# RWKV-7/Hyena block step: the scan's triangular inverse accumulates in PSUM over its levels, and Gram and output matmuls alternate between the two heads of a block

## What is computed

```python
def step(s, inp):
    r_t, w_t, k_t, v_t, kk_t, a_t = inp
    sa = jnp.einsum('bhvk,bhk->bhv', s, -kk_t)
    s = (s * w_t[:, :, None, :] + sa[..., :, None] * (kk_t * a_t)[..., None, :]
         + v_t[..., :, None] * k_t[..., None, :])
    return s, jnp.einsum('bhvk,bhk->bhv', s, r_t)
```

## Time and profile before

| | |
|---|---|
| Runs of the kernel before | 2445.35, 2448.92, 2464.73 us (median 2448.92) |
| Profiled execution: span | 2456.2 us (its own time is known only as this span, 7.3 us above the median) |
| Mean granted TensorE clock | 0.908 of full speed |
| PE busy | 2161.2 us, 88% of the span |
| PE weight load busy | 1846.5 us, 75% |
| DVE busy | 1120.2 us, 46% |
| ACT busy | 816.9 us, 33% |
| First layer's scan | about 204 to 620 us |
| Second layer's scan | about 1071 to 1466 us |
| L802, seeds of GM | 96 matmuls of 512 columns |
| L807, seeds of DM | 80 matmuls of 512 columns |

### The profile page before, as it was taken

The page is one execution under the profiler, slowest core; times in us unless marked ns, Lnnn a source line. Parts: engine busy times, 40 slices in busy tenths (PEclk is TensorE's granted clock), DMA queues, the critical chain, the costliest instruction groups (busy, mean ns, idle before and its releaser), DMA issues. The chain is left out here.

```text
span 2456.2 us, 31677 instructions
## 1 busy us (share of the span) xinstructions
PE 2161.2 (88%) x13765; PEld 1846.5 (75%) x13765; DVE 1120.2 (46%) x1369; ACT 816.9 (33%) x957; POOL 114.9 (5%) x161
## 2 busy tenths in 40 slices
PE   7888999989677998878888886778999999999996
PEld 2386776766566997768777774668899899898895
DVE  0154443232556554633444435654455454454554
ACT  0143232333223443332323323224333343343343
POOL 2001100010002000010101100000000000000000
PEclk9997999999798999856789887979999999999998
DMA  9831232232315555310101012234555655555552
GB/s 293 270 110 35 87 104 87 87 104 88 120 35 164 178 188 176 112 34 18 35 27 45 20 51 69 69 103 138 192 168 172 197 174 181 183 168 191 176 169 89
DMA packets 247418, 301.31 MB, mean 123 GB/s; under 512 B 8427, under 2 KB 224080, under 8 KB 247152
## 3 DMA queue, kind: packets, MB, share of 16 engines
q1 hardware_dynamic: 240112, 286.28, 36.4%
q0 software_dynamic: 4192, 11.28, 1.5%
q10 hardware_dynamic: 2976, 1.73, 0.2%
HBM read 297.69 MB, written 1.57 MB: 122 GB/s over the span
## 5 line engine op out<-in xcount | busy, mean ns | idle before, releaser
L1326 DVE TENSOR_TENSOR WL<-WRING,WH 128x2048 fp32r<-128x2048 f32 (+1 forms) x237 | 516.2, 2179 | 565.7 <-ACT WH L1063 564.2
L639 PE MATMUL PS<-HTH,WH 128*128 128x256 f32 x2448 | 721.4, 295 | 39.1 <-issue 22.1
L641 PE MATMUL PS<-HTH,WL 128*128 128x256 f32 x2448 | 708.1, 289 | 0.0
L640 PE MATMUL PS<-HTL,WH 128*128 128x256 f32 x2448 | 708.0, 289 | 0.0
L1063 ACT ACTIVATE WH<-WRING 128x2048 fp32r<-128x2048 f32 (+1 forms) x237 | 431.4, 1820 | 697.9 <-PE PS L641 444.9
L639 PEld LDWEIGHTS PS<-HTH,WH 128*128 128x128 f32 x2448 | 482.0, 197 | 53.2 <-issue 42.6
L640 PEld LDWEIGHTS PS<-HTL,WH 128*128 128x128 f32 x2448 | 480.4, 196 | 0.2
L641 PEld LDWEIGHTS PS<-HTH,WL 128*128 128x128 f32 x2448 | 478.8, 196 | 0.0
L673 PE MATMUL PS<-WRING,CONDT 128*2 128x256 f32 x768 | 192.2, 389 | 6.3 <-DMA WRING<-in_w_ada 6.0
L952 PE MATMUL PS<-WH,AH 128*128 128x512 f32 x440 | 171.8, 391 | 13.0 <-DVE WL L1326 13.0
L1178 ACT ACTIVATE GM<-PS 128x512 fp32r<-128x512 f32 x112 | 66.7, 597 | 325.6 <-PE PS L804 325.4
(11 more groups left out here) (331 smaller groups left out, 2561.4 us busy)
## 6 DMA issues: line engine op xcount, KB each, us to landing
WRING<-in_exp_w_in SPq DMA_DIRECT2D x80, 1024.0 KB, 5.4
WRING<-in_w_ada SPq DMA_DIRECT2D x48, 1024.0 KB, 5.2
WRING<-in_w_in SPq DMA_DIRECT2D x42, 1024.0 KB, 5.4
WRING<-in_exp_w_out SPq DMA_DIRECT2D x40, 1024.0 KB, 4.9
WRING<-in_ffn_w_in SPq DMA_DIRECT2D x22, 1024.0 KB, 5.2
WRING<-in_ffn_w_out SPq DMA_DIRECT2D x11, 1024.0 KB, 4.9
WRING<-in_w_o SPq DMA_DIRECT2D x8, 1024.0 KB, 5.0
WRING<-in_exp_w_in SPq DMA_DIRECT2D x16, 512.0 KB, 3.9
```

What stands on the lines that cost most here:

```text
L639: mm(out, h[:, kb, c], hi[:, kb, :], start=kb == 0, stop=False)
L640: mm(out, h[:, kb, c], lo[:, kb, :], start=False, stop=False)
L641: last = mm(out, s[:, kb, c], hi[:, kb, :], start=False, stop=kb == k - 1)
L1326: tt(WL[:, m % 2, 0:k * w], WRING[:, n % RING, 0:k * w], WH[:, m % 2, 0:k * w].bitcast(F32), ALU.subtract)\
```

## The change

The seeds of levels 1 to 6 (GM) and 1 to 5 (DM) go: since nothing else writes `bk[0]` and `bk[1]` between the levels, the matrices stay in PSUM, and each update adds its four products to them. Only level 0 keeps its identity seeds. The copies to GM and DM stay.

The Grams are made in pairs of the two heads: step 1 makes s = 0 and 2 in `bk[0]` and `bk[2]`, step 2 makes s = 1 and 3 in `bk[1]` and `bk[0]`, and within a pair the four matmuls alternate between the heads. DVE's masked copies follow that order, two per step. All four transposes now stand in step 3. The output matmuls of step 22 alternate between the heads in the same way. No instruction of another engine is added or removed.

```diff
-                def gram(s, bank):
-                    r = slice(HD * (s // 2), HD * (s // 2) + HD)
-                    ar = AR[x][r, s % 2, :, :].rearrange("p a t -> p (a t)")
-                    mm(PS[:, bank, 0:256], BK[x][r, 0, s % 2, :], ar, start=True, stop=True)
-                    return mm(PS[:, bank, 256:512], BK[x][r, 1, s % 2, :], ar, start=True, stop=True)
+                def gram_pair(g, banks):
+
+                    for m in range(2):
+                        for hh in range(2):
+                            r = slice(HD * hh, HD * hh + HD)
+                            ar = AR[x][r, g, :, :].rearrange("p a t -> p (a t)")
+                            last = mm(PS[:, banks[hh], m * 256:(m + 1) * 256], BK[x][r, m, g, :], ar, start=True, stop=True)
+                            if m == 1:
+                                last.then_inc(ev(f"gram{x}"), 1)
...
-                    for s in range(3):
-                        last = gram(s, bk[s])
-                        last.then_inc(ev(f"gram{x}"), 1)
+                    gram_pair(0, (bk[0], bk[2]))
                 elif step == 2:
                     pe.wait_ge(ev(f"masked{x}"), 4 * j + 1)
-                    gram(3, bk[0]).then_inc(ev(f"gram{x}"), 1)
+                    gram_pair(1, (bk[1], bk[0]))
+                elif step == 3:
                     pe.wait_ge(ev(f"masked{x}"), 4 * j + 3)
-                    for s in range(3):
+                    for s in (0, 2, 1):
                         pe.transpose(four(bk[1], s), MAT[x][:, s, 0, :], IDENT[:, :])
-                elif step == 3:
                     pe.wait_ge(ev(f"masked{x}"), 4 * j + 4)
...
-                    g_, d_ = (GM[x][:, :, :], DM[x][:, :, :]) if lv else (unit, unit)
-                    mm(PS[:, bk[0], :], IDR[:, :], g_, start=True, stop=False, skip_group_check=True)
+                    d_ = DM[x][:, :, :] if lv else unit
+                    if lv == 0:
+                        mm(PS[:, bk[0], :], IDR[:, :], unit, start=True, stop=False, skip_group_check=True)
                     for s in range(4):
                         last = mm(four(bk[0], s), d_[:, s, :], XS[x][:, s, :], start=False, stop=True, skip_group_check=True)
                     last.then_inc(ev(f"update{x}"), 1)
                     if lv < LEVELS - 1:
-                        mm(PS[:, bk[1], :], IDR[:, :], d_, start=True, stop=False, skip_group_check=True)
+                        if lv == 0:
+                            mm(PS[:, bk[1], :], IDR[:, :], unit, start=True, stop=False, skip_group_check=True)
...
+                    for g in range(G):
+                        for part in range(3 if g else 2):
+                            for hh in range(2):
+                                q = 2 * hh + g
...
-                    for s in ((0, 1, 2) if step == 1 else (3,)):
-                        dve.wait_ge(ev(f"gram{x}"), 4 * j + s + 1)
+                    g = step - 1
+                    for hh in range(2):
+                        s, bank = 2 * hh + g, (bk[0], bk[2])[hh] if g == 0 else (bk[1], bk[0])[hh]
+                        dve.wait_ge(ev(f"gram{x}"), 4 * j + 2 * g + hh + 1)
```

More of the change, by code:

```diff
@@ L831, in scan @@
                     pe.wait_ge(ev(f"solved{x}"), (j + 1) * (NREF + 1))
[L832 to L841, removed]
+                    for g in range(G):
+                        for part in range(3 if g else 2):
+                            for hh in range(2):
+                                q = 2 * hh + g
+                                v = slice((2 * blk + hh) * HD, (2 * blk + hh + 1) * HD)
+                                o = PS[HD * hh:HD * hh + HD, bk[0], g * T:(g + 1) * T]
+                                if part == 0:
+                                    mm(o, UU[x][:, q, :], MAT[x][:, q, 1, :], start=g == 0, stop=False, skip_group_check=True)
+                                elif part == 1:
+                                    last = mm(o, VT[:, g, v], MAT[x][:, q, 3, :], start=False, stop=g == 0, skip_group_check=True)
+                                else:
+                                    last = mm(o, S0P[x][:, hh, :], AR[x][:, 1, 1, :], start=False, stop=True, skip_group_check=True)
                     last.then_inc(ev(f"y_ps{x}"), 1)
@@ L1479, in scan @@
                         dve.wait_ge(ev("zeros"), 4 * l + 4)
-                    for s in ((0, 1, 2) if step == 1 else (3,)):
-                        dve.wait_ge(ev(f"gram{x}"), 4 * j + s + 1)
+                    g = step - 1
+                    for hh in range(2):
+                        s, bank = 2 * hh + g, (bk[0], bk[2])[hh] if g == 0 else (bk[1], bk[0])[hh]
+                        dve.wait_ge(ev(f"gram{x}"), 4 * j + 2 * g + hh + 1)
                         dve.copy_predicated(MAT[x][:, s, :, :].rearrange("p m t -> p (m t)"),
-                                            MASKS[:, d, :, :].rearrange("p m t -> p (m t)"), PS[:, bk[s % 3], :])\
+                                            MASKS[:, d, :, :].rearrange("p m t -> p (m t)"), PS[:, bank, :])\
                             .then_inc(ev(f"masked{x}"), 1)
```

## The result

The changed kernel takes 2389.9 us (median of four runs, 2381.9 to 2399.9) where the kernel before took 2455.2 us on the same chip (four runs): a ratio of 0.9742, 95% interval 0.9691 to 0.9792. Compared again on another chip, with more runs, it is 0.971 (0.9666 to 0.9753). That is 63 to 71 us less. The forecast was 2415 us with a range of 2379 to 2443, and a gain of 34 us: the direction and the range held, the size was half of what came. The measured time lies in rival B's stretch (2379 to 2401), outside that of my own account A (2401 to 2428).

A forecast was written before the change was run, and what follows sets the result against it. TensorE's own instructions were taken to bound both scans. 47 + 23 + 10 = 80 us off, less 19 for waits and 27 for clock, gave 34 us: 2415 us, range 2379 to 2443.

The forecast's parts named there:

- rival B: Whole kernel: the clock stays as it is, only 19 us are lost, gain 61 or 70 us, 2379 to 2401; chance 0.25.
- my own account A: Whole kernel: second scan has a third more low time, give or take half; gain 21 to 48 us, 2401 to 2428; chance 0.43.
- What bounds the kernel, and that removed work reaches the end: Both scans: mostly bound by TensorE's own instructions, so time removed there reaches the end, less new waits and clock loss.
- Seeds, 47 us: Both scans: 176 seeds go, 144 at 0.21 us and 32 at 0.54 us; 47 us, bounds 37 and 95.
- Grams and outputs, 33 us: Steps 1 and 22 of each block: four Gram passes go, 23 us; six output pass times go, 10 us.
- Rival E: Grams and outputs: the pairs do not overlap, so the time is 2449 or a little more; chance 0.04.
- What is added: Both scans: lost cover turns into new waits, four terms together 19 us, between 5 and 35.
- Term (a): Step 3 now waits for both masks of step 2: 5 blocks of 16 at 1 us, 5 us.
- term (b): Behind an update, the copy of GM loses three seeds' cover; half shows in the 15 starved places, 5 us.
- term (c): First scan: waits for adaLN rows grow and some new ones come, 4 us.
- term (d): Masked product late because DVE is at a weight tile: seeds removed ahead of it buy only waiting, 5 us.
- The clock, 27 us: Second scan: without seeds, low-clock time grows by a third, 58 us on 174, losing 27 us.

The follow-up runs named there:

- change_again: The changed kernel itself, run once more beside its parts; 0.971 of the kernel before, median 2384.0 us.
- seeds_only: The kernel before with the 176 seeds of levels 1 and up removed and nothing else; 0.9884 of the kernel before, 28 us less.
- the warm pair: The kernel before, with and without its seeds, both with unread identity matmuls ahead of the waits for factors; 0.9851 and 0.9722 of the kernel before.
- pairs_only: The changed kernel with all its seeds put back, leaving the Gram pairs and alternating outputs; 0.9858 of the kernel before, 35 us less.
- no_fill: The changed kernel with no fills in the second layer's scan, its eleven projection tiles placed behind the scan; 0.9898 of the kernel before.

## Why the prediction was right or wrong

**What bounds the kernel, and that removed work reaches the end: right.** Busy time in the scans fell by 71 us and idle time rose by 3.6; in change_again's execution they are 84 and 3.9.

**Seeds, 47 us: the pitches were right.** The half update takes the 0.45 to 0.48 us that was forecast. In the trace of before 34 seeds started low, where I had worked out 32. With the loss of clock counted as above, the pitches give 24 us for seeds_only and 27 for the warm pair, and 28 and 31.5 were measured.

**Grams and outputs, 33 us: right.** pairs_only measured 35 (24 to 46). An output step gives 0.70 us against a forecast of 0.65, and a block's Grams lose the four passes of step 1. Rival E is refuted, and so is the strict order of matmuls for these tiles.

**The waits, 19 us: the step "What is added" was mis-sized.** Idle time grew by 3.6 us. Term (a), 5 us, was 1.8; term (b), 5 us, was about 1; term (c), 4 us, was 0.6; term (d), 5 us, was 1.7 (22.2 to 23.9). The wait at the Grams that the profile calls "issue" fell by 2.7 us, which pays for part of them. For (b) I had let each of the 15 starved places show half of the lost cover as a new wait. Only three places show one, each right ahead of a wait for XS, as here:

```profile
1084.41 0.82 PE L793 MATMUL PS<-GM,AS 128*128 128x128 f32 x4 [0.24 <-ACT GM L1184]
1086.01 1.12 PE L807 MATMUL PS<-XS,DM 128*128 128x128 f32 x4 [0.79 <-DVE XS L1507]
```

In the other twelve the copy of GM was done in time. For (d) no run tells how many of the removed seeds stood ahead of a late product; 1.7 us is what came.

**The clock, 27 us: the mechanism was right and its size, for the whole change, was not.** I forecast 58 us more low time in the second scan, on 174. Its clock stayed at 0.77 (0.78 in change_again) over a scan 42.5 us shorter, so the low time fell, to about 161 us. The prediction had named a clock that does not go down by a few hundredths as a sign of being wrong, and that sign came. Over the program the low time is 437 against 454 us. That seeds hold some of the clock is shown by one comparison and suggested by another: seeds out with the stalls filled, 25 us more low time; seeds out alone, 34 us more, with as much noise. What I left out is the other side: the pairs take out work that ran mostly at the low level, and low time fell by 30 us with them, of which 19 are their own passes. I had those 19 us in the Gram term, and the seeds' 17 in theirs, and then charged the clock on top of an unchanged 174. Why the remaining 11 go, and why the seeds' loss is smaller beside the pairs (13 us from pairs_only to change_again) than alone (34), the runs don't settle: the clock of seeds_only alone ranges from 0.893 to 0.909 over six runs, which is 83 us of low time.

**The sum.** 80 us off TensorE; the waits took 4. Low time fell by 17 us in all, where the low share of the removed work alone (17 us of seeds, 19 us of Gram passes) would have lowered it by 36: 19 us of other work moved to the low level, 9 us of time. 80 - 4 - 9 = 67 us; measured 63 and 71. The 17 and so the 9 are within the noise; what the sum shows is that the clock's term is near 10 us and not 27. **The forecast failed in preferring A to B**: the trace showed why a clock might fall, and I priced it without the part of the change that raises it. Waits and clock were charged 46 us and cost 13. That the time is inside the range owes to the room left for B and not to my account.

## What to carry to other kernels

Where an engine is busy nine tenths of a stretch, price removed work by start-to-start distances at each clock level and expect nearly all of it back; new waits should be charged only where the removed instruction stands inside the cover of a particular wait, which the timeline shows. Look for two matmuls on different halves of the array and put them within a few instructions of each other; for the Grams here the exact order did not matter, and for the outputs it gave 0.27 of 0.70 us a block. TensorE's clock is a resource that dense work earns for the thin work around it: filling a stall with matmuls whose results nobody reads gave 37 us in the kernel before and 10 to 18 on top of the change, and cutting the same filler work into smaller runs lost 19 to 27.

## What the runs showed of the hardware

- A matmul on one half of the array's rows starts beside an earlier group on the other half, four passes ahead of it in the program: eight Gram passes took 2.09 us in either order, against 3.7 us for twelve before. On halves of the columns it does so only in part: an output step took 1.51 us with each head's matmuls together inside a group, 1.24 alternating and 1.94 before.
- TensorE stayed at 1.2 GHz for 109 us while it was busy 92 of them, and through 32.1 us of small matmuls without a gap (no_fill).
- The seeds, though pure copying, kept some of the clock: with the stalls filled, the second scan ran at 0.89 with its 88 matmuls of 512 columns and at 0.84 without, and the time at the low level was 25 us less over the program.
